# The experts' down weights asked for by ScalarE on its own queue, gate and up weights by SP

## The reference, cut to what matters

```python
xb = hf[toks]
hid = jax.nn.silu(jnp.matmul(xb, w_g[e])) * jnp.matmul(xb, w_u[e])
return jnp.matmul(hid, w_d[e]) * wb[:, None]
```

## Time and profile before

| | us |
|---|---|
| median of 3 runs | 2888.19 |
| the runs | 2883.37 to 2891.59 |
| the profiled execution | 2894.49 |
| its span, first to last instruction | 2892.7 |

### The profile page before, as it was taken

The page is one execution under the profiler, slowest core; times in us unless marked ns, Lnnn a source line. Parts: engine busy times, 40 slices in busy tenths (PEclk is TensorE's granted clock), DMA queues, the critical chain, the costliest instruction groups (busy, mean ns, idle before and its releaser), DMA issues.

```text
span 2892.7 us, 36287 instructions
## 1 busy us (share of the span) xinstructions
PE 2731.9 (94%) x13214; PEld 2237.7 (77%) x13214; DVE 1961.8 (68%) x2336; ACT 1467.5 (51%) x2228; POOL 519.7 (18%) x394
## 2 busy tenths in 40 slices
PE   7999999999988999999989998999999899999996
PEld 6788978788766777888878877778778788888875
DVE  6776756565654653435544987899763799888885
ACT  5544436443335664443333457533422477777774
POOL 0001400000126773001000000000010044334431
PEclk9999999999999999999999999999999899999998
DMA  5712066743786762121211100112232799999995
GB/s 173 261 49 73 1 194 244 279 157 132 278 243 173 155 137 62 51 102 44 96 58 47 51 23 1 37 44 68 78 104 81 270 381 377 375 362 369 362 360 170
DMA packets 189469, 471.85 MB, mean 163 GB/s; under 512 B 74353, under 2 KB 74481, under 8 KB 164496
## 3 DMA queue, kind: packets, MB, share of 16 engines
q1 hardware_dynamic: 166112, 427.86, 43.5%
q10 hardware_dynamic: 14000, 25.30, 2.4%
q0 software_dynamic: 9216, 16.81, 2.3%
HBM read 410.84 MB, written 75.83 MB: 168 GB/s over the span
## 4 chain that ended last, share of the span: by engine, by line
PE 51%; DMA 13%; DVE 8%; POOL 6%; issue 5%; ACT 4%; SPq 0%; POOLq 0%; DVEq 0%; ACTq 0%; PEldq 0%
PE ps L906 7%; PE ps L908 7%; PE ps L907 7%; DMA ex_raw<-in_w_up_e 6%; POOL fa_pl L1938 6%; DMA ex_raw<-in_w_down_e 5%; PE ps L1354 5%; PE ps L1356 5%; PE ps L1357 5%; PE ps L3515 3%; DVE ex_w L3665 3%; ACT ex_w L3600 2%; PE ps L3243 1%; PE ps L2618 1%; PE ps L2276 1%
## 5 line engine op out<-in xcount | busy, mean ns | idle before, releaser
L3665 DVE TENSOR_TENSOR ex_w<-ex_raw,ex_w 128x2048 fp32r<-128x2048 f32 x190 | 430.6, 2289 | 64.6 <-ACT ex_w L3600 62.3
L3600 ACT ACTIVATE ex_w<-ex_raw 128x2048 fp32r<-128x2048 f32 x190 | 361.9, 1916 | 112.9 <-DMA ex_raw<-in_w_up_e 63.0
L3515 PE MATMUL ps<-ex_w,ex_xT 128*128 128x512 f32 x1536 | 368.0, 396 | 12.6 <-DVE ex_xT L3680 12.3
L3515 PEld LDWEIGHTS ps<-ex_w,ex_xT 128*128 128x128 f32 x1536 | 286.8, 189 | 79.2 <-issue 14.0
L798 DVE SCALAR_TENSOR_TENSOR arena<-arena,small 128x1023 f32<-128x1023 f32 (+9 forms) x168 | 213.4, 1270 | 3.7
L1938 POOL TENSOR_TENSOR fa_pl<-fa_p,fa_ph 128x512 fp32r<-128x512 f32 x192 | 196.3, 1040 | 84.6 <-ACT fa_ph L2040 82.8
L1480 DVE TENSOR_TENSOR bs_b<-arena,bs_b 128x512 fp32r<-128x512 f32 x160 | 110.3, 690 | 139.5 <-ACT bs_b L1378 139.2
L1378 ACT ACTIVATE bs_b<-arena 128x512 fp32r<-128x512 f32 x160 | 100.1, 629 | 201.6 <-PE ps L1357 180.0
L3515 PE MATMUL ps<-ex_w,ex_hT 128*128 128x512 f32 x768 | 184.2, 396 | 1.3 <-issue 1.0
L3515 PEld LDWEIGHTS ps<-ex_w,ex_hT 128*128 128x128 f32 x768 | 142.8, 189 | 31.6 <-issue 2.6
L1755 DVE TENSOR_REDUCE small<-ps 128x1 f32<-128x512 f32 (+1 forms) x192 | 101.1, 553 | 84.6 <-PE ps L1734 56.4
(11 more groups left out here) (466 smaller groups left out, 6688.8 us busy)
## 6 DMA issues: line engine op xcount, KB each, us to landing
ex_raw<-in_w_gate_e SPq DMA_DIRECT2D x64, 1024.0 KB, 13.8
ex_raw<-in_w_up_e SPq DMA_DIRECT2D x64, 1024.0 KB, 13.6
ex_raw<-in_w_down_e SPq DMA_DIRECT2D x64, 1024.0 KB, 14.1
bs_a<-h_ops SPq DMA_DIRECT2D x100, 512.0 KB, 4.2
arena<-in_w_in SPq DMA_DIRECT2D x72, 512.0 KB, 3.7
arena<-in_w_in SPq DMA_DIRECT2D x18, 1024.0 KB, 6.8
h_ops<-ko_s SPq DMA_DIRECT2D x16, 512.0 KB, 6.1
h_ops<-xbc_t SPq DMA_DIRECT2D x16, 512.0 KB, 4.0
```

The source lines that it names most:

```text
L3515: mm = nc.tensor.matmul(out, l, r, start=(k == 0 and n == 0), stop=(k == kc - 1 and n == 2))
L3600: nc.scalar.activation(half_of(part[m][0], h), raw[m][:, h * W // 2: (h + 1) * W // 2], ACT.Identity).then_inc(high[m], 1)
L3665: V.tensor_tensor(half_of(part[m][1], h), raw[m][:, h * W // 2: (h + 1) * W // 2], half_of(as_f32(part[m][0]), h), ALU.subtract)\
```

## The change

SP no longer asks for the down weights, except those of the last expert. ScalarE asks for them, on its own queue: at the head of its cycle, ahead of `silu`, it waits for each half of the low down weights of the expert before and issues the DMA. The wait is on the same semaphore with the same value as before on SP, and the buffer and the semaphore of the landing are the same.

```diff
@@ def sync(sp): def cycle(now, before, after) @@
                 for h in range(2):
                     sp.wait_ge(low[GATE], 2 * NE + 2)
                     load_half(sp, [raw[GATE]] * 3, experts, NE - 1, [last_loaded] * 3, DOWN, h)
-            elif now and now is not FIRST:
-                load(*now, (DOWN,))
 
@@ def scalar(act) @@
+        def load_down(i, s):
+            b = i * ns + s
+            for h in range(2):
+                act.wait_ge(low[DOWN], b * 2 + (h + 1))
+                load_half(act, raw, experts, b, loaded, DOWN, h)
+
         def cycle(now, before, after):
             if before is LAST:
                 take_y(*before, bank=0)
                 return
+            if not extra and now and now is not FIRST and now is not LAST:
+                load_down(*now)
             if now:
                 silu(*now)
             if before:
```

## The result

| | before | after |
|---|---|---|
| median us | 2888.12 | 2918.64 |
| runs | 2883.37 to 2891.59 | 2913.10 to 2922.99 |
| span of the profiled execution | 2892.7 | 2918.1 |

The ratio is 1.0106 with a 95% interval of 1.0083 to 1.0129: 1.1% slower, 30.5 us by the medians, 25.4 us by the two spans. The forecast was 27.8 us more and a median of 2916.0.

A forecast was written before the change was run, and what follows sets the result against it. TensorE was taken to bound the expert stage until 2476, transfers after. A new ScalarE-VectorE loop of 19.27 us a cycle adds 29.0 us by P(31), the last cycle saves 1.2: +27.8, median 2916.0 us, range 2896 to 2934.

The forecast's parts named there:

- Nothing gained on SP: SP's queue: two DMAs less per cycle, 0.33 us each, release no other request; 0 us.
- The step from VectorE to `silu`: ScalarE, from VectorE's end of the low down pair to `silu`: registers, DMA, dispatch; 0.65 us, bounds 0.43 and 0.9.
- The loop, 19.27: Closed chain through VectorE and ScalarE, once around per expert cycle, including the new step: 19.27 us, bounds 19.05 and 19.52.
- P(2) at 2316.15, P(31) at 2875.0: Starts of TensorE's first gate products of experts 2 and 31, 29 cycles apart; before 2314.82 and 2846.01.
- The last cycle 1.2 us shorter: Last expert cycle, without the new step: up weights arrive in time, so VectorE's last low parts start 1.2 us sooner.
- The transfers lose their backlog: Weight loads need about 18.5 us a cycle, under 19.27, so landings stay nearer 7 to 8 us than 14.
- a DMA share clearly under 1.00: Sign that the forecast is right: the expert stage's DMA share falls clearly below the earlier 1.00.
- The median: Whole kernel: +27.8 us, 2916.0 us, 1.0% slower, with the profiled execution's 6.3 us above its median carried over.
- The rule to weigh: DMA engines go round robin between queues, so down halves would overtake earlier up and gate halves; no change in time.
- the covered wait: Rival 1: ScalarE's wait is covered and transfers after 2476 stay the limit; not slower, 2888 us, chance 0.08.
- The faster case: Rival 2: a separate down queue improves transfers, TensorE's 17.75 us cycles hold to the end; 2872 us, chance 0.04.
- The late down half: Rival 3: shared bandwidth makes a down half 0.7 us late each cycle, cycles of 20.0; 2937 us, chance 0.08.

The follow-up runs named there:

- e7: Changed kernel with each down half asked for by two DMAs of 0.5 MB, two more issues per cycle on ScalarE; 2938.0 us, ratio 1.0165.
- e9: Changed kernel with both down waits and requests on ScalarE moved behind the high up weights, ahead of `take_y`; 2952.6 us, ratio 1.0230.
- e5: Kernel before, with each down load from expert 1 on cut to a quarter of its half, all computing kept; 2871.2 us, ratio 0.9929.
- e6: Changed kernel with each down load from expert 1 on cut to a quarter of its half; 2917.6 us, ratio 1.0084 to the kernel before.
- e4: Changed kernel, but ScalarE waits and asks for the first down half only, SP asks for the second; 2891.2 us, ratio 1.0004.
- e3: Changed kernel with ScalarE's down waits and requests moved behind `silu` and `hi_h`, ahead of the high gate weights; 2892.0 us, ratio 1.0004.
- e2: Kernel before, SP asking for all weights, with only ScalarE's wait for both low down halves added ahead of `silu`; 2902.7 us, ratio 1.0043.
- e1: Changed kernel with ScalarE's down requests moved behind both high gate weights, ahead of `hi_x`; 2894.7 us, ratio 1.0014.
- e8: Changed kernel with the first down request behind `hi_h`, the second behind the first high gate weights, both on ScalarE; 2893.0 us, ratio 1.0008.

## Why the prediction was right

The forecast was 2916.0 with a range of 2896 to 2934; measured 2918.6. By its steps:

- **Nothing gained on SP**: right. With two requests less, gate and up requests still wait for VectorE.
- **The step from VectorE to `silu`, 0.65 us**: 0.61. The second request leaves 0.16 us after its wait ends, the DMA takes 0.34, near SP's 0.33, and not the 0.53 of the upper bound, and 0.11 follow. Line 1431, which gave that bound, is a DMA right behind another, as the long one of e7 is; in e9 such a one takes 0.34, so the 0.53 stays unexplained. The bounds of the step, 0.43 and 0.9, are also wider than the two bounds of the DMA make them, 0.57 and 0.83.
- **The loop, 19.27**: 19.21 on VectorE. The terms that did not contain the new step were pitches from rows of before, and they held to 0.01 us each: 4.48, 2.91, 5.01, 1.14, 5.06.
- **P(2) at 2316.15, P(31) at 2875.0**: 2316.43 and 2873.25. TensorE's idle time is 1.2 us a cycle (22.1 of 364 us) and not 1.5: the loop is 0.07 shorter, and a gate product behind a wait takes 5.74 us where it took 5.61; the rest was not followed up.
- **The last cycle 1.2 us shorter**: the span ends 44.85 us after P(31), before 46.7, so 1.8. The last low parts start 9.93 us after P(31), 10.15 expected, 11.31 before; that explains 1.4 of the 1.8.
- **The transfers lose their backlog**: landings of 7.6 us in the median, as in the earlier trace rows. But "a DMA share clearly under 1.00" was wrong: it is 0.98 to 0.99. The sign took for granted that the share shows a limit. e5 shows that the 1.00 of the earlier trace rows had a limit behind it, and e6 that the 0.98 of the changed kernel has none.
- **The median**: 30.5 us against 27.8. The spans differ by 25.4. The profiled execution of before was among its slower ones (2894.49 for a median of 2888), which I carried over as a constant 6.3 us; the profiled one of after lies only 1.3 above its median. The kernel before depends on how transfers fall and its late cycles vary from 17.9 to 19.2, the loop's do not; that this makes the difference is argued, not shown. So the 2.6 us by which the median was missed are in part luck: the span was forecast 2.4 us too long, and the 6.3 us carried over happened to be about 5 too many for the changed kernel.
- **The rule to weigh**: that a down half on a queue of its own would overtake others. In the changed kernel it did not: down halves land in 8.4 us in the median over the whole stage, gate and up halves in 7.6 and 7.5. e4 and e3 above point in opposite directions. It changed nothing in the time, as forecast.
- **The rivals**: the covered wait (2888) falls by e2, which has the wait alone and is slower. The faster case falls by e1: with the wait out of the way a second queue brings nothing. The late down half (2937) did not occur at the head of the cycle, where no wait for DMA is left; e9 shows that it exists where the request comes late. Its latest landing was worked out 0.2 us too early: 26.5 - 1.9 is P + 24.6, which leaves 14.9 us and not 14.6.

By the Trainium skill ("DMA: Bandwidth & Descriptors", section "Issuing engines are not separate DMA queues") issuing from two engines saves only issue time; e1 and e8 agree that a second queue brings no bandwidth that shortens the kernel, with 1.0014 and 1.0008.

## What to carry to other kernels

Before a request is moved to an engine that computes, write down where its wait would end in that engine's cycle, and where the engine stands at that time: the request is free as long as the instructions ahead of it keep the engine busy past that moment, and costs the whole gap (and the DMA's issue too) where they don't. It can go out well before its place in the program, since the sequencer runs ahead of the engine. A second engine's wait on the first closes a loop; add up its terms once around from the rows, and compare the sum with the present cycle, since only what exceeds it is lost. Compare with what each limit would allow by itself: here the kernel held by its transfers hides 0.6 us a cycle (18.3 for 17.75) of what a change costs elsewhere.

## What the runs showed of the hardware

- ScalarE's sequencer runs ahead of its engine. A DMA goes out before instructions that stand ahead of it in the program have started: both requests before the second high gate part in 28 of 30 cycles of e1, and before the second high up part in all 30 of e9.
- The time of a DMA on ScalarE's sequencer: 0.34 us for 1 MB with over 2 us between two (the changed kernel). In e7 three of four DMAs of 0.5 MB took that, the last of the four 0.34 to 0.89. In e9 two of 1 MB follow each other with 0.23 us between them in the cycle shown above, and none takes more than 0.45:

```profile
L3325 ACTq DMA_DIRECT2D ex_raw<-in_w_down_e x52: 339/339/443, 2306.5 to 2813.8; - x52
```

- The DMA share does not tell a limit. At 364, 351 and 270 GB/s it was 1.00, 0.98 and 0.81 (before, changed, e6), and only behind the first of these the transfers held the pace; e1, with the pace of the kernel before, has 0.98 too, at 365 GB/s. What told more here was the time from issue to landing, 14.1 us against 7.6 in the first two, and best the run with fewer bytes.
